# Four projections of the second block as seven half-size products each, with x parked in DRAM

## The reference, cut to what matters

```python
h = rmsnorm(x, norm1_w[l]) * (1.0 + scale1) + shift1
proj = h @ w_in[l]
(q_m, k_m, v_m, o_m, i_pre, f_pre, q_d, k_d, v_d, g_m, g_d) = jnp.split(proj, split_idx, axis=-1)

qk = jax.nn.silu(causal_conv(jnp.concatenate([q_m, k_m], axis=-1), conv_w[l], conv_b[l]))
...
hm = mlstm_chunkwise(qh, kh, vh, log_i, log_f).astype(x.dtype)
...
qd = partial_rope(rmsnorm(qd, q_norm_w[l]), positions)
kd = partial_rope(rmsnorm(kd, k_norm_w[l]), positions)
...
hd = diff_attention(qd, kd, vd, lam)
...
merged = jax.nn.sigmoid(g_m) * (hm @ w_br_m[l]) + jax.nn.sigmoid(g_d) * (hd @ w_br_d[l])
x = x + gate1 * (merged @ w_out[l])
```

## Time and profile before

| | |
|---|---|
| median of 3 runs | 1375.59 us (1373.51 to 1376.93) |
| the profiled execution: time | 1383.87 us |
| the profiled execution: span | 1382.0 us |
| PE busy | 1257.8 us, 91% of the span |
| DVE busy | 536.8 us, 39% |
| ACT busy | 319.2 us, 23% |
| POOL busy | 206.2 us, 15% |
| DMA | 208.79 MB, mean 151 GB/s |

### The profile page before, as it was taken

One profiled execution on the slowest core, in us unless ns is written; L12 is line 12 of the kernel. 1 busy time (PEld: TensorE's weight loads), 2 busy tenths in 40 slices (PEclk: granted clock), 3 DMA queues, 4 the chain that ended last, 5 costly groups with the idle time before them and its releaser, 6 DMA issues.

```text
span 1382.0 us, 12804 instructions
## 1 busy us (share of the span) xinstructions
PE 1257.8 (91%) x4712; PEld 654.2 (47%) x4712; DVE 536.8 (39%) x1438; ACT 319.2 (23%) x739; POOL 206.2 (15%) x198
## 2 busy tenths in 40 slices
PE   7799989999989999999999896899999969977785
PEld 3455434445544444744444443677774534432331
DVE  3114473566377622124702357422222533211221
ACT  4213553433300002133222343310000321100110
POOL 6000023354300000000000002322300021211100
PEclk9999999999999999999988996999999979999998
DMA  9525131332375330342110110011228479999992
GB/s 316 103 69 122 61 91 32 107 123 92 107 239 187 121 123 1 122 146 97 61 61 0 62 54 8 1 61 61 61 67 364 163 293 400 403 408 405 408 365 77
DMA packets 91524, 208.79 MB, mean 151 GB/s; under 512 B 20105, under 2 KB 51097, under 8 KB 79639
## 3 DMA queue, kind: packets, MB, share of 16 engines
q1 hardware_dynamic: 77936, 186.79, 37.1%
q0 software_dynamic: 10176, 17.96, 5.4%
q10 hardware_dynamic: 3344, 3.16, 0.7%
HBM read 203.60 MB, written 12.66 MB: 156 GB/s over the span
## 4 chain that ended last, share of the span: by engine, by line
PE 69%; SPq 11%; DVE 9%; DMA 4%; ACT 3%; issue 2%; POOL 0%; POOLq 0%; DVEq 0%; ACTq 0%
SPq L2550 10%; PE PS L2086 7%; PE PS L1555 6%; PE PS L962 6%; PE PS L1377 4%; PE PS L1455 4%; PE PS L1600 4%; PE PS L2145 3%; PE PS L2234 3%; PE PS L607 3%; PE PS L2665 3%; PE PS L1386 2%; PE PS L1838 2%; PE PS L1567 2%; PE PS L677 2%
## 5 line engine op out<-in xcount | busy, mean ns | idle before, releaser
L962 PE MATMUL PS<-HT,W 128*128 128x512 f32 x256 | 126.0, 616 | 1.8 <-ACT AN L1126 1.7
L1224 POOL TENSOR_SCALAR AN<-AN,SM 128x128 f32<-128x128 f32 (+3 forms) x64 | 72.2, 1135 | 202.6 <-DVE SM L1316 202.6
L2665 PE MATMUL PS<-AN,HT 128*64 128x512 f32 x272 | 83.5, 629 | 18.3 <-DMA AN<-in_w_up 8.8
L1555 PE MATMUL PS<-W,HT 128*128 128x512 f32 x192 | 90.2, 630 | 0.0
L1247 DVE SCALAR_TENSOR_TENSOR AN<-AN,COLA 128x256 f32<-128x256 f32 x168 | 85.1, 507 | 5.0
L2051 POOL TENSOR_TENSOR AN<-HT 128x1024 f32<-128x1024 f32 x1 | 2.4, 2411 | 480.7 <-DVE AN L1877 480.7
L607 PE MATMUL PS<-W,HT 128*128 128x512 f32 (+1 forms) x192 | 70.5, 528 | 0.0
L2744 DVE TENSOR_TENSOR HT<-HT,PS 128x256 f32<-128x256 f32 x16 | 6.7, 421 | 150.7 <-ACT HT L2722 150.7
L962 PEld LDWEIGHTS PS<-HT,W 128*128 128x128 f32 x256 | 45.0, 195 | 39.7 <-issue 36.1
L1555 PEld LDWEIGHTS PS<-W,HT 128*128 128x128 f32 x192 | 38.8, 205 | 47.4 <-issue 47.3
L2665 PEld LDWEIGHTS PS<-AN,HT 128*64 128x64 f32 x272 | 27.7, 145 | 70.4 <-issue 68.3
(11 more groups left out here) (487 smaller groups left out, 2028.1 us busy)
## 6 DMA issues: line engine op xcount, KB each, us to landing
W<-in_w_in SPq DMA_DIRECT2D x14, 2048.0 KB, 9.2
W<-in_w_down SPq DMA_DIRECT2D x20, 1024.0 KB, 23.8
AN<-in_w_ada SPq DMA_DIRECT2D x17, 1024.0 KB, 5.3
AN<-in_w_gate SPq DMA_DIRECT2D x15, 1024.0 KB, 19.4
AN<-in_w_up SPq DMA_DIRECT2D x15, 1024.0 KB, 29.1
AN<-in_w_down SPq DMA_DIRECT2D x12, 1024.0 KB, 21.4
W<-in_w_gate SPq DMA_DIRECT2D x10, 1024.0 KB, 22.6
W<-in_w_up SPq DMA_DIRECT2D x10, 1024.0 KB, 29.2
```

The source lines that it names most:

```text
L962: t = pe.matmul(u.ap, w[:, c, tile(m)], hT[:, c, :], start=c == 0, stop=c == 7)
L1555: t = pe.matmul(u.ap, hT[:, c, tile(i)], wv(slot, 8, 512)[:, c, :], start=c == 0, stop=c == 7)
L2665: t = pe.matmul(u.ap[r, :].rearrange("p (n f) -> p n f", n=2), XGT[e % 2][:, c, r], w_gu(3 * e + half)[:, c], start=c == 0, stop=c == 7)
```

## The change

- **Seven products of halves.** Rotary k (`kd`), the convolution's q (`cm0`), its k (`cm1`) and mLSTM's v (`va`) are each computed by `pe_half`, seven products x = 1, 6, 2, 5, 3, 7, 4. One takes 8 products of 128x128 by 128x256 (features on the partitions for cm0 and cm1, tokens for kd and va) into one bank.
- **Sums on POOL.** A new `pool_block2` makes the four sums T of `hT` right after `hT` is complete, and then four sums of 128x1024 for each of the four weight blocks. The sums T are no longer made in `pool_halves`.
- **x waits in DRAM.** The sums T have their place in `X`. SP writes each of the four tiles of x to `scr_x` after its residual is done (`sp_spill`), and reads them back in `sp_merge2`, ahead of the second half of `w_out_2`. `dve_residual` waits for the tile.
- **Putting together on DVE.** ACT copies product 1 (`act_half`), DVE adds the other six (`dve_half`, 7 operations of one PSUM and one SBUF input for each block). In cm0 and cm1 the results land in two rows of `CB`, one of them in `OM`, one behind `WIQ`, and the convolution reads both.
- **Order on DVE and ACT.** The first rotation (of q) is done while kd is put together, the second one under cm0; the convolutions follow in pairs. The silus follow on ACT in pairs.
- **Loads.** cm1 has slot 2 now (slot 0 holds sums of weights), and is loaded together with va when kd is done.

The core of the diff:

```diff
-    CB = [omf[:, 516 * n:516 * n + 516] for n in range(2)]
+    CB = [omf[:, 0:1030], WIQ[:, 3072:4102]]
...
-    TS = [omf[:, 1024 * n:1024 * n + 1024].rearrange("p (c t) -> p c t", c=4) for n in range(2)]
-    TS.append(half_t[1])
-    TS.append(fv(VA[:, 0, 1, 0:1], [[516, 4], [1, 256]]))
+    TS = [X[:, 1024 * n:1024 * n + 1024].rearrange("p (c t) -> p c t", c=4) for n in range(4)]
+    WH = [[W[s][:, 1024 * x:1024 * x + 1024].rearrange("p (c f) -> p c f", c=4) for x in range(3)] for s in range(2)]
...
+    def sp_spill(sp, ws, i):
+
+        ws.wait_ge(*B.use("wo", i, 0).out)
+        ws.wait_ge(*B.use("wo", i, 1).out)
+        sp.dma_start(xd[tile(i), :], xs[:, i, :]).then_inc(*x_spilled[i].up())
...
+    HALVES = (("kd", 2, 1, True), ("cm0", 3, 0, False), ("cm1", 2, 0, False), ("va", 1, 0, True))
...
+        for i, (a, b) in enumerate(((b12, b11), (b22, TS[0]), (b22, b12), (b21, TS[1]))):
+            wg.wait_ge(*x_spilled[i].at())
+            wg.wait_ge(*on_act.at("xT2", "sum", i))
+            wg.wait_ge(*on_dve.at("xT2", "xn", i))
+            step(("T", i + 1), pool.tensor_tensor(TS[i], a, b, ALU.subtract))
+        earlier = None
+        for name, slot, place, _ in HALVES:
+            a11, a12, a21, a22 = half_w(slot)
+            s1, s2, s4 = WH[place]
+            wg.wait_ge(*ring[slot].at(name))
+            if name == "kd":
+                wg.wait_ge(*B.use("pb", 7).full)
+            elif name == "cm0":
+                wg.wait_ge(*B.use("qd", 3, 1).full)
+            else:
+                wg.wait_ge(*B.use(earlier, 6).full)
+                wg.wait_ge(*B.use(earlier, 5).full)
+            step((name, 1), pool.tensor_tensor(s1, a21, a22, ALU.add))
+            step((name, 2), pool.tensor_tensor(s2, s1, a11, ALU.subtract))
+            if name in ("cm1", "va"):
+                wg.wait_ge(*B.use(earlier, 3).full)
+            step((name, 4), pool.tensor_tensor(s4, a12, s2, ALU.subtract))
+            step((name, 3), pool.tensor_tensor(a21, a11, a21, ALU.subtract))
+            earlier = name
...
+        for half in range(2):
+            r = slice(128 * half, 128 * half + 128)
+            for c in range(4):
+                if tokens:
+                    m = pe.matmul(u.ap[:, 256 * half:256 * half + 256], t[:, c, r], s[:, c, :], start=c == 0, stop=c == 3)
+                else:
+                    m = pe.matmul(u.ap[:, 256 * half:256 * half + 256], s[:, c, r], t[:, c, :], start=c == 0, stop=c == 3)
+        m.then_inc(*u.filled)
...
-        for i in range(1, NT):
-            pe_tokens2(pe, wp, "kd", 2, i)
...
+        for x in (6, 2, 5, 3, 7, 4):
+            pe_half(pe, wp, "kd", x)
+        for name in ("cm0", "cm1", "va"):
+            for x in (1, 6, 2, 5, 3, 7, 4):
+                pe_half(pe, wp, name, x)
...
         for n in range(2):
             ws.wait_ge(*B.use("prod", 2 + n, 1, 4).full)
+            if n:
+                for i in range(NT):
+                    ws.wait_ge(*x_spilled[i].at())
+                    sp.dma_start(xs[:, i, :], xd[tile(i), :]).then_inc(*x_back[i].up())
             sp.dma_start(wv(2 + n, 8, 512), wsrc(A["w_out_2"][0], 512 * n, 512)).then_inc(*ring[2 + n].up("wo2", n))
...
-        step(("T", 1), pool.tensor_tensor(TS[0], b12, b11, ALU.subtract))
-        step(("T", 2), pool.tensor_tensor(TS[1], b22, TS[0], ALU.subtract))
-        step(("T", 3), pool.tensor_tensor(TS[2], b22, b12, ALU.subtract))
-        wg.wait_ge(*B.use("mv", 3, 3).full)
-        step(("T", 4), pool.tensor_tensor(TS[3], b21, TS[1], ALU.subtract))
...
     def dve_residual(dve, wd, i, n):
+        wd.wait_ge(*x_back[i].at())
```

More of the change, by code:

```diff
@@ L399, in build @@
     line_out, line_back, xn_out = sig("line_out", "line_back", "xn_out", step=16)
+    x_spilled = sig(*[f"x{i}_spilled" for i in range(NT)], step=16)
+    x_back = sig(*[f"x{i}_back" for i in range(NT)], step=16)
     x_out = sig("x_half0_out", "x_half1_out", step=16)
@@ new lines, in act_half, with dve_half @@
+    def act_half(act, wa, name):
+        u = B.use(name, 1)
+        wa.wait_ge(*u.full)
+        act.activation(half_dst(name)[0], half_src(u, name), ACT.Copy).then_inc(*u.read)
+    def dve_half(dve, wd, name, x):
+        c11, c12, c21, c22 = half_dst(name)
+        u = B.use(name, x)
+        v = half_src(u, name)
+        wd.wait_ge(*u.full)
+        if x == 6:
+            wd.wait_ge(*B.use(name, 1).out)
+            if name == "cm1":
+                wd.wait_ge(*qk_dve.at(3, 3))
+            dve.tensor_tensor(c21, v, c11, ALU.add).then_inc(*u.read)
+        if x == 2:
+            wd.wait_ge(*B.use(name, 6).out)
+            dve.tensor_tensor(c11, v, c11, ALU.add).then_inc(*u.read)
+        if x == 5:
+            wd.wait_ge(*B.use(name, 6).out)
+            dve.tensor_tensor(c12, v, c21, ALU.add).then_inc(*win2_dve.up(name, "U4"))
+        if x == 3:
+            wd.wait_ge(*win2_dve.at(name, "U4"))
+            dve.tensor_tensor(c12, v, c12, ALU.add).then_inc(*u.read)
+        if x == 7:
+            wd.wait_ge(*win2_dve.at(name, "U4"))
+            dve.tensor_tensor(c21, v, c21, ALU.add).then_inc(*u.read)
+            wd.wait_ge(*u.out)
+            u = B.use(name, 5)
+            dve.tensor_tensor(c22, half_src(u, name), c21, ALU.add).then_inc(*u.read)
+        if x == 4:
+            wd.wait_ge(*B.use(name, 5).out)
+            dve.tensor_tensor(c21, v, c21, ALU.add).then_inc(*u.read)
@@ new lines, in dve_block2 @@
+    def dve_block2(dve, wd):
+        dve.memset(VA[:, :, :, 128:129], 1.0).then_inc(*set_dve.up("va"))
+        for a in range(2):
+            if a:
+                wd.wait_ge(*B.use("qd", 3, 1).full)
+            for n in range(2):
+                dve.memset(CB[a][:, 515 * n:515 * n + 3], 0.0).then_inc(*set_dve.up("zero", a, n))
+        dve_half(dve, wd, "kd", 6)
+        dve_gates2(dve, wd)
+        for x in (2, 5, 3):
+            dve_half(dve, wd, "kd", x)
+        dve_rotate_sum(dve, wd, 0)
+        dve_half(dve, wd, "kd", 7)
+        dve_rotate(dve, wd, 0)
+        dve_half(dve, wd, "kd", 4)
+        dve_rotate_sum(dve, wd, 1)
+        dve_half(dve, wd, "cm0", 6)
+        dve_half(dve, wd, "cm0", 2)
+        dve_rotate(dve, wd, 1)
+        for g, name in enumerate(("cm0", "cm1")):
+            if g:
+                dve_half(dve, wd, name, 6)
+                dve_half(dve, wd, name, 2)
+            dve_half(dve, wd, name, 5)
+            dve_half(dve, wd, name, 3)
+            dve_conv2(dve, wd, 4 * g)
+            dve_conv2(dve, wd, 4 * g + 1)
+            dve_half(dve, wd, name, 7)
+            dve_half(dve, wd, name, 4)
+            dve_conv2(dve, wd, 4 * g + 2)
+            dve_conv2(dve, wd, 4 * g + 3)
+        for x in (6, 2, 5, 3, 7, 4):
+            dve_half(dve, wd, "va", x)
```

161 lines of the change are left out of this document (95 added, 66 removed).

## The result

| | before | after |
|---|---|---|
| median of 8 runs each | 1376.26 us (1372.57 to 1381.09) | 1385.12 us (1381.19 to 1389.36) |
| ratio | | 1.0062, interval 1.0036 to 1.0088 |
| profiled execution, span | 1383.87, 1382.0 us | 1387.88, 1386.1 us |

The change makes the kernel 0.6% slower, where the prediction had 16 us less and 0.95 on faster. The two traces split the difference by stage. Each stage runs from the first PE instruction of its kind to the next stage's. The sum is the difference of the spans, +4.1 us.

The account below looks back on a forecast made before the run. PE's products were taken to bound the projections, DVE the middle of the difference attention. 13.3 - 0.5 + 3.2 = 16.0 us off the median 1375.6 gave 1359.6 us, range 1356 to 1367.

Parts of the forecast that it names:

- The products: Projections, 589.4 to 700.2 us: PE's stretch takes 97.5 instead of 110.8 us, 13.3 us less.
- The banks: Projections: PE waits 0.5 us in all for PSUM banks that DVE must read first; bounds 0 and 7.
- DVE is the bound: Rival, projections: PE waits at cm1 3 and va 3, which give 6 to 8 us; 1364 to 1366 us, chance 0.22.
- two tight places: Projections, cm1 3 and va 3: PE wants banks of cm1's and cm0's product 5, margins under a microsecond.
- The sums T: Difference attention: without POOL's four sums there, DVE's path is 3.2 us shorter; bounds 2.5 and 4.5.
- x comes back: Reads of x ahead of w_out_2's second half: hidden from both waiters, counted 0, upper bound 2 us.
- The start of mLSTM: After the projections: moves by what PE's stretch gives, first product at about 692.3 instead of 705.57 us.
- Slower, by the clock: Rival, cm1 3 to mLSTM's start: repeated stalls drop PE to 1.2 GHz; 1411 us, chance 0.03.
- The saving is made but not kept: Rival: another wait in the difference attention, or the tail takes 3 to 5 us back; 1362 to 1365 us, chance 0.1.

## Why the prediction was wrong, point by point

- **The products: right.** 13.3 us were counted, 13.17 measured, and every group of 16 follows after 3.45 us.
- **The banks: right.** 0.5 us were counted and none was lost; the rival "DVE is the bound" is out. The two tight places, after:

```profile
650.32 0.69 DVE L1675 TENSOR_TENSOR W<-PS,W 128x512 f32<-128x512 f32 x1
```

```profile
652.44 3.62 PE L1642 MATMUL PS<-HT,W 128*128 128x256 f32 x16
```

```profile
674.94 0.69 DVE L1675 TENSOR_TENSOR W<-PS,W 128x512 f32<-128x512 f32 x1
```

  cm1 3 was said to want its bank at 652.4 and to get it at 652.1; L1675, the last to read that bank, ends at 651.01, and PE goes on at 652.44 without idle time. The margin was 1.4 us and not 0.3. cm1 5 was said to be read at 676.0 to 676.5; it was read by 675.63, and PE went on at 676.61 without idle time. The rotation of k was to be some 8 us longer than 7.2. Its steps after, POOL's sums beside them:

```profile
629.58 4.33 DVE L1819 TENSOR_TENSOR AN<-AN,SM 128x2048 f32<-128x2048 f32 x1
633.94 7.78 DVE L1822 TENSOR_TENSOR AN<-AN,SM 128x256 f32<-128x256 f32 x4
```

```profile
628.60 3.16 POOL L1612 TENSOR_TENSOR W<-W 128x1024 f32<-128x1024 f32 x1 [29.23 <-PE PS L1642]
631.84 4.28 POOL L1613 TENSOR_TENSOR W<-W 128x1024 f32<-128x1024 f32 x1
```

  From its reciprocal at 626.88 to 642.52 it took 15.6 us, 8.4 more. In the convolution under va's sums the tensor_scalar waited as well:

```profile
651.84 0.55 DVE L1853 TENSOR_SCALAR AN<-W,COLB 128x512 f32<-128x512 f32 x1
652.42 6.27 DVE L1857 SCALAR_TENSOR_TENSOR AN<-W,COLB,AN 128x512 f32<-128x512 f32 x3
658.62 2.57 DVE L1853 TENSOR_SCALAR AN<-W,COLB 128x512 f32<-128x512 f32 x1
```

  2.57 us for 0.55, while POOL's third sum of va ran from 658.23 to 660.91. The Trainium skill (SBUF — State Buffer, Who interferes with whom) says that a tensor_scalar in a 2-port mode takes the port pair too; the prediction had no row for it, and this one agrees.
- **The sums T: right.** 3.2 us were counted; PE's idle time fell from 7.24 to 4.05 us, 3.19 less, and the whole stage by 4.04, inside the bounds of 2.5 to 4.5.
- **x comes back: here the prediction failed.** It named two waiters of SP's queue, the first residual and the second half of w_out_2, found both hidden (both were: the residual waited for PE, not for x), added that the experts' first loads are pushed back and made up for, and concluded "I count 0, and 2 us as the upper bound". The term measured +31.3 us: 26.8 of it are PE's longer wait for the router's small loads (27.34 for 0.58), and 4.1 the half clock behind it. It looked along SP's queue only. The four loads that ACT issues 7 us later than x's reads use the same 16 engines, and they were nowhere in the sum or among the rivals. The trace of before had the warning: PE waited 0.58 us for just these loads, so they had no slack at all, and they had 2.4 us of start on ten loads of 1 MB. An upper bound of 2 us had to cover every load in flight in that stretch, and not the longest ones alone.
- **The start of mLSTM: not seen.** That "the start of mLSTM moves by what PE's stretch gives" is 13 us in the forecast; its own idle time and half clock (10 us in the traces) were taken as given. The change of the bank rotation can be read from the code: the banks of the last transposes shift by four. The effect of the matmuls' form could not.
- **The rivals.** "Slower, by the clock" (0.03) came to the right side by a mechanism that did not happen: the clock was 1.00 over the whole stretch. "The saving is made but not kept" (0.1) was the right kind, and looked for the loss in the experts' weights at 3 to 5 us; it was in front of them and six times that.
- **The number that came out.** With the small loads moved, the kernel takes 1359.22 us, 0.4 from the forecast of 1359.6. That is luck, and no confirmation of the sum: the traces of before and after give 27 us up to w_out_2, of which 16.4 are the terms counted and 10 the start of mLSTM, which was not; the early issue takes some 4.8 back; and the medians give 17.8. Of the five traces with the start of mLSTM as in before, four have 78 to 82 us for it and one 72.6, so one pair of traces doesn't tell what the clock gives in the median.

## What to carry to other kernels

Before a transfer is added to or moved along a queue, list everything that is in flight in that stretch on all queues, the smallest loads first, and for each how long its user already waits; a load with an idle time of 0.58 us ahead of its user has no slack, however few bytes it has. Small loads of many packets belong where the engines are free, long before they are needed: moved ahead of the merge, 0.17 MB went from 32 us of landing to 3, and that turned 0.6% slower into 1.4% faster. The issue itself has a price too: here it held ACT for 2.2 us on the path and the traces show 4.8 us for it, so a place where the issuing engine is idle should be better still (not tried). Code that changes the number of banks taken also changes who waits at the next stage; the first product after it is the place to read in the trace.

## What was not expected of the hardware

- 0.17 MB in 2368 packets landed within 5.3 us when the engines were free and took up to 32.4 us beside loads of 1 MB on another queue, at one small packet of some 90 bytes for each large one of 7.3 KB (1344 to 1343 in 24 us, 1128 to 1131 in 20 us of another kernel). Issuing the third of the four loads kept ACT for 12.57 us, and for 0.59 to 0.95 where the engines were free.
- A tensor_scalar of DVE with one input in SBUF took 2.57 us for 0.55 under a sum of POOL (one row). POOL's sums beside DVE's rotation took up to 4.28 us for 2.35.
- An idle time of 1.06 us of PE was followed by 10 to 14 us at a granted clock of 0.5 (1.2 GHz) in all five traces with matmuls of 512 columns over the stretch ahead, and by none in the three with 256 columns, PE being busy without a gap over the stretch ahead in both.
